# Epsilon moved into the square root's bias, and one quarter of the last token tile normalised by ScalarE and GpSimd beside VectorE

## The chip, the cores and the metric

The kernel runs on one core of one Trainium2 chip. The metric is the time of one execution in microseconds; the kernel before takes 941.61 us, the median of three runs (941.43 to 941.96).

## The reference, cut to what matters

One decoder layer: input projections, dilated window attention, a pooling mixer, gates, an output projection, and at the end a layer norm over the sum of the scaled input and the projection. The change touches only the layer norm:

```
out = jnp.einsum('bsd,de->bse', merged, w_out)
xf = DEEPNORM_ALPHA * x + out
mu = jnp.mean(xf, axis=-1, keepdims=True)
var = jnp.mean(jnp.square(xf - mu), axis=-1, keepdims=True)
y = (xf - mu) * lax.rsqrt(var + LN_EPS) * gamma + beta
```

The 256 tokens lie in two tiles of 128 partitions (t = 0 and 1); a token's row has 2048 columns, worked on as four blocks of 512 (c or b = 0 to 3).

## The kernel before, in words

Three stages stream 1 MB chunks of weights through a ring of three slots. ScalarE rounds each chunk to its high part, VectorE subtracts to get the low part, and TensorE multiplies both. Stage A makes the heads and the mixers, stage B the gates and the merged branches, stage C the output projection with its layer norm. All orders are written out by hand, one program for each engine, tied by semaphores.

In stage C, VectorE adds the scaled input to each finished block (`add_rows`), takes its statistics (`statistics`) and multiplies it by gamma at once (`times_gamma`), while TensorE works on the next block. For the last block, TensorE makes tile 0 first and then the two halves of tile 1 (`last_half`). So tile 0 is finished and stored while TensorE still computes, and what follows TensorE's last product is tile 1 alone:

- `last_half(1)`: adding the rows (L1078), statistics (L1080), `variance` with `bn_aggr` (L1089) and the addition of epsilon (L1090), and the product with gamma of the last 256 columns (L1084).
- ScalarE's square root (L808), VectorE's reciprocal (L1095) and the shift, which is minus the mean times that reciprocal (L1102).
- The shift's parts for TensorE (L1102, L1170). TensorE turns them into rows (L667), ScalarE copies these out of PSUM (L810), and TensorE multiplies them with rows of gamma and beta (L672). This gives shift times gamma plus beta of a whole block in PSUM, for blocks 1 to 3.
- VectorE makes block 0 by itself (`normalise_here`: L1110 for shift times gamma plus beta, L1112 for the result), and then blocks 1, 2 and 3 by one instruction each with the operand from PSUM (`normalise_rows`: L1119).
- SP stores each block of 256 KB as `out_ready` rises (L392), in the order of the blocks, and waits at the end until all have landed.

Ahead of the roots ScalarE loads the table for the square root by a root of a constant (L804). GpSimd has no work in this kernel.

Of the kernel before, what the change touches and what calls it, by code (L numbers as in the profile page):

```python
# [22 lines left out]
F32 = mybir.dt.float32  # L23
F32R = mybir.dt.float32r
ALU = mybir.AluOpType
ACT = mybir.ActivationFunctionType
# [14 lines left out]
LN_EPS = 1e-5  # L41
# [4 lines left out]
TT = SEQ // P  # L46
# [74 lines left out]
BLOCK = 512  # L121

ROWS = 5
BLOCKS = D_MODEL // BLOCK
BLOCK_CHUNKS = OT // BLOCKS
BLOCK_KT = KT // BLOCK_CHUNKS
# [35 lines left out]
def layer_kernel(nc, first_d, x_d, stream_d, bias_d, scale_d, gamma_d, rows_d, row_kind_d, ident_d, mask_d,  # L162
                 coef_d, inv_d, beta_d, out_d):
    with ExitStack() as ctx:
        def sem(name):
            return ctx.enter_context(nc.semaphore(name))
# [7 lines left out]
        base = nc.sbuf_base - 206 * 1024  # L174
        base = (base + 31) // 32 * 32

        def place(at, items):
            made = []
            for name, shape, dt in items:
                made.append(nc.alloc_sbuf_tensor_at(name, [P] + shape, dt, offset=at))  # L180
                at += 4 * int(np.prod(shape))
            return at, made

        at, (xt, w_raw, w_hi, w_lo, ident, coef, gate_bias, half_bias, pool_scale,
             nmax, smax, den, rden, stats, mv, rstd, shift_parts, shift,
             row_kind) = place(base, [
                 ("xt", [KT, 2, SEQ], F32R),
                 ("w_raw", [RING, CHUNK], F32), ("w_hi", [RING, CHUNK], F32R),
                 ("w_lo", [RING, CHUNK], F32R), ("ident", [P], F32),
# [2 lines left out]
                 ("nmax", [8], F32), ("smax", [8], F32), ("den", [8], F32), ("rden", [8], F32),  # L192
                 ("stats", [TT, 2 * BLOCKS, 6], F32), ("mv", [TT, 8], F32), ("rstd", [8], F32),
                 ("shift_parts", [TT, 8], F32), ("shift", [8], F32),
                 ("row_kind", [8], F32)])
        at_ya = at + (base - at) % LINE
        skew = LINE - (at_ya - at)
        at, (ya,) = place(at_ya, [("ya", [HEADS, 2, SEQ], F32R)])
# [34 lines left out]
            ("rows_hi", [D_MODEL], F32), ("rows_signed", [D_MODEL], F32)])  # L233
        _, (shift_rows, row_parts) = place(at_szp, [
            ("shift_rows", [TT, P], F32R), ("row_parts", [D_MODEL], F32R)])
        _, (last_hi, last_lo, beta, shifted) = place(base, [
            ("last_hi", [CHUNK], F32R), ("last_lo", [CHUNK], F32R), ("beta", [D_MODEL], F32),
            ("shifted", [2, BLOCK], F32)])

        _, (corr_pair, pair_f) = place(at_szp, [("corr_pair", [2, SEQ], F32), ("pair_f", [2, SEQ], F32)])  # L240
        assert max(end_a, end_b) <= nc.sbuf_usable_end, (end_a, end_b, nc.sbuf_usable_end)
# [28 lines left out]
        tail_landed = sem("tail_landed")  # L270
# [39 lines left out]
        norm_shift_ready = sem("norm_shift_ready")  # L310
        vec = sem("vec")
        var_ready = sem("var_ready")
        std_ready = sem("std_ready")
        shift_ready = sem("shift_ready")
        out_ready = sem("out_ready")
        out_landed = sem("out_landed")

        N_CONSTS = 6
        CONSTS = 16 * N_CONSTS

        block = ctx.enter_context(nc.Block())
# [41 lines left out]
        @block.sync  # L363
        def _(sp):
            def load(slot, chunk):
                sp.dma_start(w_raw[:, slot, :], stream_d[chunk, :, :]).then_inc(raw_landed[slot], 16)

            for q, (before, upto) in enumerate(PIECES):
                lies = slice(P * before * PIECE_COLS, P * upto * PIECE_COLS)
                sp.dma_start(piece_raw(q), first_d[lies].rearrange("(p c) -> p c", p=P)).then_inc(piece_landed[q], 16)  # L370
            for slot in range(RING):
                load(slot, RING + slot)
            for dst, src in ((mask[:, :, :], mask_d), (ident[:, :], ident_d), (coef[:, :], coef_d),
                             (gate_bias[:, :], bias_d), (pool_scale[:, :], scale_d), (inv[:, :, :], inv_d)):
                sp.dma_start(dst, src).then_inc(consts_landed, 16)
            whole = (CHUNKS - RING) // RING
            with sp.Fori(1, whole) as i:
                for j in range(RING):

                    sp.wait_ge(lo_split, i * (2 * RING) + 2 * (j + 1))  # L380
                    sp.dma_start(w_raw[:, j, :],
                                 stream_d[bass.ds(i * RING + (RING + j), 1), :, :]
                                 .rearrange("a p n -> (a p) n")).then_inc(raw_landed[j], 16)
            for n in range(RING * (whole + 1), CHUNKS):
                sp.wait_ge(lo_split, 2 * (n - RING + 1))
                load(n % RING, n)

            for n in range(TT * BLOCKS):

                sp.wait_ge(out_ready, n + 1)  # L390
                t, cols = n // BLOCKS, slice(n % BLOCKS * BLOCK, (n % BLOCKS + 1) * BLOCK)
                sp.dma_start(out_d[t, :, cols], res[:, t, cols]).then_inc(out_landed, 16)  # L392
            sp.wait_ge(out_landed, 16 * TT * BLOCKS)


        @block.tensor
        def _(pe):
# [268 lines left out]
            pe.wait_ge(shift_ready, 1)  # L666
            turn(value_ps[0:ROWS, 0:P], shift_parts[:, 1, 0:ROWS], ident[:, :]).then_inc(row_turned, 1)  # L667

            pe.wait_ge(rows_split, 1)
            pe.wait_ge(shift_rows_ready, 1)  # L670
            for c in range(1, BLOCKS):
                mm(norm_shift(c)[:, :], shift_rows[0:ROWS, 1, :], row_parts[0:ROWS, c * BLOCK:(c + 1) * BLOCK],  # L672
                   start=True, stop=True).then_inc(norm_shift_ready, 1)

# [2 lines left out]
        def _(act):  # L677
            activation = nc.scalar.activation
# [98 lines left out]
            with act.Fori(0, B_STEPS) as i:  # L777
                for j in range(B_CHUNKS):
                    split_hi(B_FIRST, j + AHEAD, i, B_CHUNKS)
                    correction(B_FIRST, j, i, B_CHUNKS, pair=j % 3 == 2)  # L780
                    if j % 3 < 2:
# [3 lines left out]
                                   bias=half_bias[:, bass.ds(i * 4 + ((j % 3) * OT + j // 3), 1)],  # L785
                                   scale=0.5).then_inc(tanh_done, 1)
# [13 lines left out]
            for half in range(2):  # L800
                cols = slice(half * HALF * P, (half + 1) * HALF * P)
                activation(last_hi[:, cols], w_raw[:, (CHUNKS - 1) % RING, cols], ACT.Copy).then_inc(hi_split, 1)

            activation(rstd[:, 4:5], ident[:, 0:1], ACT.Sqrt)  # L804
            for t in range(TT):

                act.wait_ge(var_ready, t + 1)
                activation(rstd[:, t:t + 1], mv[:, t, 2:3], ACT.Sqrt).then_inc(std_ready, 1)  # L808
            act.wait_ge(row_turned, 1)
            activation(shift_rows[0:ROWS, 1, :], value_ps[0:ROWS, 0:P], ACT.Copy).then_inc(shift_rows_ready, 1)  # L810


        @block.vector
        def _(dve):
            tt, ts = nc.vector.tensor_tensor, nc.vector.tensor_scalar
# [17 lines left out]
            chain = Chain()  # L833
# [233 lines left out]
                chain.add(nc.vector.bn_stats(stats[:, t, c, :], res[:, t, c * BLOCK:(c + 1) * BLOCK]))  # L1067

            def times_gamma(c, t):
                at = res[:, t, c * BLOCK:(c + 1) * BLOCK]  # L1070
                chain.add(tt(at, at, gamma[:, c * BLOCK:(c + 1) * BLOCK], ALU.mult))

# [13 lines left out]
            def variance(t):  # L1086

                chain.ready()
                chain.link(nc.vector.bn_aggr(mv[:, t, 0:2], stats[:, t, 0:BLOCKS + t, :].rearrange("p a s -> p (a s)")))  # L1089
                ts(mv[:, t, 2:3], mv[:, t, 1:2], LN_EPS, None, ALU.add).then_inc(var_ready, 1)  # L1090

            def token_rstd(t):

# [12 lines left out]
            def normalise_here(t, c):  # L1106

                cols = slice(c * BLOCK, (c + 1) * BLOCK)
                at = res[:, t, cols]
                chain.link(stt(out=shifted[:, c % 2, :], in0=gamma[:, cols], scalar=shift[:, t:t + 1],  # L1110
                               in1=beta[:, cols], op0=ALU.mult, op1=ALU.add))
                stt(out=at, in0=at, scalar=rstd[:, 2 + t:3 + t], in1=shifted[:, c % 2, :],  # L1112
                    op0=ALU.mult, op1=ALU.add).then_inc(out_ready, 1)

            def normalise_rows(t, c):

                dve.wait_ge(norm_shift_ready, c)
                at = res[:, t, c * BLOCK:(c + 1) * BLOCK]
                stt(out=at, in0=at, scalar=rstd[:, 2 + t:3 + t], in1=norm_shift(c)[:, :],  # L1119
                    op0=ALU.mult, op1=ALU.add).then_inc(out_ready, 1)  # L1120

            def split_rows():
                chain.link(copy(rows_hi[0:ROWS, :].bitcast(F32R), rows[0:ROWS, :]))
                chain.link(ts(rows_signed[0:ROWS, :], rows_hi[0:ROWS, :], row_kind[0:ROWS, 1:2], None, ALU.mult))
                stt(out=row_parts[0:ROWS, :], in0=rows[0:ROWS, :], scalar=row_kind[0:ROWS, 0:1],
                    in1=rows_signed[0:ROWS, :], op0=ALU.mult, op1=ALU.add).then_inc(rows_split, 1)

            chain.link(nc.vector.memset(shift_parts[:, :, :], 1.0))
            for e in range(OT - 1):
                if e + AHEAD < OT - 1:  # L1130
                    split_lo(C_FIRST, e + AHEAD, 0, 0)
                if e + AHEAD == OT - 1:
                    for half in range(2):
                        cols = slice(half * HALF * P, (half + 1) * HALF * P)
# [3 lines left out]
                if e % BLOCK_CHUNKS == BLOCK_CHUNKS - 1:  # L1138
                    c = e // BLOCK_CHUNKS
# [15 lines left out]
            c = BLOCKS - 1  # L1155
# [8 lines left out]
            for b in range(BLOCKS):  # L1164
# [4 lines left out]
            token_shift(1, True)  # L1169
            tt(shift_parts[:, 1, 2:3].bitcast(F32R), shift[:, 1:2], shift_parts[:, 1, 0:1],  # L1170
               ALU.subtract).then_inc(shift_ready, 1)
            normalise_here(1, 0)
            for b in range(1, BLOCKS):
                normalise_rows(1, b)


# [113 lines left out]
```

## Time and profile before

| what | value |
|---|---|
| median of the runs | 941.61 us (941.43 to 941.96) |
| span of the profiled execution, first to last instruction | 939.3 us |
| own time of the profiled execution | not recorded apart from its span |
| median of the runs less that span | 2.3 us |
| TensorE busy | 932.3 us, 99% |
| VectorE busy | 634.1 us, 68% |
| ScalarE busy | 420.2 us, 45% |
| GpSimd busy | 0.2 us, 4 instructions |
| chain that ended last | TensorE 98%, VectorE 1% |

Times in the rows count from the first instruction. A row of the timeline gives start, duration, engine, line, operation, the tile written and those read, shapes, and the number of instructions merged in it. In brackets stands the idle time before it and who ended it. Instructions on VectorE that don't wait for one another start some 0.07 us before the one in front of them ends.

### The profile page before, as it was taken

To read this page: it belongs to the slowest core of one execution; us is meant where nothing else is said; L and a number is where in the kernel's file an instruction comes from. 1 tells how busy PE (TensorE), PEld (TensorE's weight loads), DVE (VectorE), ACT (ScalarE), POOL (GpSimd) and SP (SyncE) were. 2 spreads that over 40 slices of the span, in tenths; PEclk is the share of its full clock that TensorE was granted. 3 is DMA by queue.
4 is the path that set the end of the run, shared out by engine and by line. 5 is a ranking of instruction groups with operands and counts; after the bars stand their busy time and mean duration, and the time that the engine had idled before them with its cause. 6 is when DMAs were issued, how large, how long until landed. Compare 5 with 4: busy or idle time off the path is not lost.

```text
span 939.3 us, 13719 instructions
## 1 busy us (share of the span) xinstructions
PE 932.3 (99%) x5190; PEld 812.1 (86%) x5190; DVE 634.1 (68%) x1007; ACT 420.2 (45%) x589; POOL 0.2 (0%) x4
## 2 busy tenths in 40 slices
PE   9999999999999999999999999999999999999997
PEld 7888888888888888888888889888888888888887
DVE  6767657666777567557666778666666666666866
ACT  6444444444434344444444444545445454444340
POOL 0000000000000000000000000000000000000000
PEclk9999999999999999999999999999999999999999
DMA  9745554544545545554544546655545555557432
GB/s 374 266 156 180 199 188 145 209 164 165 207 152 185 185 168 174 198 185 156 197 166 181 193 166 224 224 180 210 192 179 186 178 217 179 184 193 297 179 135 90
DMA packets 26416, 178.58 MB, mean 190 GB/s; under 512 B 3327, under 2 KB 3583, under 8 KB 5759
## 3 DMA queue, kind: packets, MB, share of 16 engines
q1 hardware_dynamic: 25920, 173.72, 51.6%
q10 hardware_dynamic: 452, 4.24, 1.2%
q8 instruction: 32, 0.52, 0.2%
q14 instruction: 12, 0.10, 0.0%
HBM read 175.85 MB, written 2.10 MB: 189 GB/s over the span
## 4 chain that ended last, share of the span: by engine, by line
PE 98%; DVE 1%; DMA 0%; ACT 0%; DVEq 0%; issue 0%
PE proj_ps L411 39%; PE proj_ps L417 20%; PE attn_ps L411 7%; PE attn_ps L403 4%; PE attn_ps L404 4%; PE attn_ps L405 4%; PE attn_ps L417 3%; PE value_ps L405 3%; PE value_ps L404 3%; PE value_ps L403 3%; PE mixed_ps L404 1%; PE mixed_ps L403 1%; PE mixed_ps L405 1%; PE mixed_ps L540 1%; PE proj_ps L454 1%; PE attn_ps L484 1%
## 5 line engine op out<-in xcount | busy, mean ns | idle before, releaser
L411 PE MATMUL proj_ps<-xt,w_hi 128*128 128x512 f32 x1600 | 557.1, 392 | 0.0
L417 PE MATMUL proj_ps<-xt,w_lo 128*128 128x256 f32 x1600 | 445.5, 280 | 0.0
L839 DVE TENSOR_TENSOR w_lo<-w_raw,w_hi 128x1024 fp32r<-128x1024 f32 x314 | 369.3, 1220 | 83.0 <-ACT w_hi L682 82.6
L411 PEld LDWEIGHTS proj_ps<-xt,w_hi 128*128 128x128 f32 x1600 | 298.3, 187 | 65.1
L682 ACT ACTIVATE w_hi<-w_raw 128x1024 fp32r<-128x1024 f32 x314 | 313.6, 1051 | 59.8 <-PE mixed_ps L405 25.1
L417 PEld LDWEIGHTS proj_ps<-xt,w_lo 128*128 128x128 f32 x1600 | 302.3, 189 | 1.4
L702 ACT ACTIVATE corr<-proj_ps 128x256 f32<-128x256 f32 x102 | 39.1, 383 | 280.8 <-PE proj_ps L417 278.2
L853 DVE TENSOR_TENSOR qk_f<-proj_ps,corr 128x256 f32<-128x256 f32 x46 | 19.5, 423 | 73.0 <-ACT corr L702 73.0
L411 PE MATMUL attn_ps<-yp,w_hi 128*128 128x512 f32 x128 | 45.1, 391 | 0.0
L411 PE MATMUL attn_ps<-ya,w_hi 128*128 128x512 f32 x128 | 45.1, 391 | 0.0
L405 PE MATMUL value_ps<-w_hi,xt 128*128 128x512 f32 x96 | 37.4, 390 | 0.0
L404 PE MATMUL attn_ps<-w_lo,xt 128*128 128x512 f32 x96 | 37.4, 390 | 0.0
L403 PE MATMUL attn_ps<-w_hi,xt 128*128 128x512 f32 x96 | 37.4, 390 | 0.0
L405 PE MATMUL attn_ps<-w_hi,xt 128*128 128x512 f32 x96 | 37.4, 390 | 0.0
L404 PE MATMUL value_ps<-w_lo,xt 128*128 128x512 f32 x96 | 37.4, 389 | 0.0
L403 PE MATMUL value_ps<-w_hi,xt 128*128 128x512 f32 x96 | 37.3, 389 | 0.0
L853 DVE TENSOR_TENSOR gate_f<-proj_ps,corr 128x256 f32<-128x256 f32 x48 | 20.3, 423 | 23.9 <-ACT corr L702 23.6
L417 PE MATMUL attn_ps<-ya,w_lo 128*128 128x256 f32 x128 | 35.8, 280 | 0.0
L417 PE MATMUL attn_ps<-yp,w_lo 128*128 128x256 f32 x128 | 35.8, 280 | 0.0
L719 ACT ACTIVATE s_sb<-s_sb,nmax 128x512 f32<-128x512 f32 x16 | 11.4, 715 | 44.7 <-DVE nmax L901 44.7
L411 PEld LDWEIGHTS attn_ps<-ya,w_hi 128*128 128x128 f32 x128 | 23.9, 187 | 5.2
L411 PEld LDWEIGHTS attn_ps<-yp,w_hi 128*128 128x128 f32 x128 | 23.9, 187 | 5.2
(178 smaller groups left out, 917.8 us busy)
## 6 DMA issues: line engine op xcount, KB each, us to landing
w_raw<-in_weights SPq DMA_DIRECT2D x158, 1024.0 KB, 4.8
first_raw<-in_first SPq DMA_DIRECT2D x8, 640.0 KB, 8.3
res<-in_x_rows ACTq DMA_DIRECT2D x1, 2048.0 KB
out_rows<-res SPq DMA_DIRECT2D x8, 256.0 KB, 2.1
gamma<-in_gamma_row ACTq DMA_DIRECT2D x1, 1024.0 KB
beta<-in_beta_row ACTq DMA_DIRECT2D x1, 1024.0 KB
mask<-in_mask SPq DMA_DIRECT2D x1, 512.0 KB, 17.7
ident<-in_identity SPq DMA_DIRECT2D x1, 64.0 KB, 17.5
```

Source lines behind the costliest of these rows:

```text
L403: mm(out, a_hi, b_hi, start=first, stop=False)
L404: mm(out, a_hi, b_lo, start=False, stop=False)
L405: return mm(out, a_lo, b_hi, start=False, stop=last)
L411: mm(bank, w_hi[:, slot, k * P:(k + 1) * P], tile.rearrange("p a s -> p (a s)"), start=first, stop=False)
L417: done = mm(bank[:, SEQ:2 * SEQ], w_lo[:, slot, k * P:(k + 1) * P], tile[:, 0, :], start=False, stop=last)
L454: mm(bank, w_hi[:, n, k * P:(k + 1) * P], xt[:, k, :, :].rearrange("p a s -> p (a s)"), start=(k == 0), stop=False)
L484: mm(out[:, :, cols], q_hi[:, g, q], keys[:, g, :, q], start=True, stop=False)
L682: activation(w_hi[:, slot, cols], w_raw[:, slot, cols], ACT.Copy).then_inc(hi_split, 1)
L702: activation(corr[:, b, :], source, ACT.Copy).then_inc(act_evac, 1)
L719: activation(s_sb[:, t, :], s_sb[:, t, :], ACT.Exp, bias=nmax[:, t:t + 1], scale=SCALE, accum_out=den[:, t:t + 1]).then_inc(exp_done, 1)
L839: tt(w_lo[:, slot, cols], w_raw[:, slot, cols], w_hi[:, slot, cols].bitcast(F32), ALU.subtract).then_inc(lo_split, 1)
L853: tt(dst, source, corr[:, bank_of(n, j), :], ALU.add).then_inc(proj_free, 1)
```

## The change

Three things are done.

- Epsilon is no longer added by VectorE (L1090 goes). A column of SBUF is set to epsilon early in stage C, and both roots take it as their bias pointer. The root now reads the variance that `bn_aggr` writes.
- Block 1 of tile 1 is not multiplied by gamma ahead (`times_gamma` leaves it out), and its rows through TensorE are left out (two products at L672 instead of three). Instead ScalarE computes block times reciprocal plus shift into a new tile, `pool_shifted`; GpSimd multiplies this by gamma and then adds beta. VectorE does blocks 0, 2 and 3.
- SP stores blocks 0, 2, 1, 3 of tile 1, in this order, and waits for GpSimd ahead of block 1.

The new column of 32 bytes moves the tiles placed behind it in SBUF by as much, but for those that are aligned anew.

```diff
@@ SP
+            def store(t, b):
+                cols = slice(b * BLOCK, (b + 1) * BLOCK)
                 sp.dma_start(out_d[t, :, cols], res[:, t, cols]).then_inc(out_landed, 16)
+            for b in range(BLOCKS):
+                sp.wait_ge(out_ready, b + 1)
+                store(0, b)
+            sp.wait_ge(out_ready, BLOCKS + 1)
+            store(1, 0)
+            sp.wait_ge(out_ready, BLOCKS + 2)
+            store(1, 2)
+            sp.wait_ge(pool_out_ready, 1)
+            store(1, POOL_BLOCK)
+            sp.wait_ge(out_ready, BLOCKS + 3)
+            store(1, 3)
@@ TensorE
-            for c in range(1, BLOCKS):
+            for c in range(POOL_BLOCK + 1, BLOCKS):
                 mm(norm_shift(c)[:, :], shift_rows[0:ROWS, 1, :], row_parts[0:ROWS, c * BLOCK:(c + 1) * BLOCK],
@@ ScalarE
-            activation(rstd[:, 4:5], ident[:, 0:1], ACT.Sqrt)
+            act.wait_ge(eps_ready, 1)
+            activation(rstd[:, 4:5], ident[:, 0:1], ACT.Sqrt, bias=eps[:, 0:1])
             for t in range(TT):
                 act.wait_ge(var_ready, t + 1)
-                activation(rstd[:, t:t + 1], mv[:, t, 2:3], ACT.Sqrt).then_inc(std_ready, 1)
+                activation(rstd[:, t:t + 1], mv[:, t, 1:2], ACT.Sqrt, bias=eps[:, 0:1]).then_inc(std_ready, 1)
+            act.wait_ge(pool_shift_ready, 1)
+            activation(pool_shifted[:, :], res[:, 1, POOL_BLOCK * BLOCK:(POOL_BLOCK + 1) * BLOCK], ACT.Identity,
+                       bias=shift[:, 1:2], scale=rstd[:, 3:4]).then_inc(centred_ready, 1)
             act.wait_ge(row_turned, 1)
             activation(shift_rows[0:ROWS, 1, :], value_ps[0:ROWS, 0:P], ACT.Copy).then_inc(shift_rows_ready, 1)
@@ GpSimd
+            pool.wait_ge(tail_landed, 16 * 5)
+            pool.wait_ge(centred_ready, 1)
+            tt(pool_shifted[:, :], pool_shifted[:, :], gamma[:, cols], ALU.mult).then_inc(pool_scaled, 1)
+            pool.wait_ge(pool_scaled, 1)
+            tt(res[:, 1, cols], pool_shifted[:, :], beta[:, cols], ALU.add).then_inc(pool_out_ready, 1)
@@ VectorE
             def times_gamma(c, t):
+                if (c, t) == (POOL_BLOCK, 1):
+                    return
@@
-                chain.link(nc.vector.bn_aggr(mv[:, t, 0:2], stats[:, t, 0:BLOCKS + t, :].rearrange("p a s -> p (a s)")))
-                ts(mv[:, t, 2:3], mv[:, t, 1:2], LN_EPS, None, ALU.add).then_inc(var_ready, 1)
+                nc.vector.bn_aggr(mv[:, t, 0:2],
+                                  stats[:, t, 0:BLOCKS + t, :].rearrange("p a s -> p (a s)")).then_inc(var_ready, 1)
@@
-                dve.wait_ge(norm_shift_ready, c)
+                dve.wait_ge(norm_shift_ready, c - POOL_BLOCK)
@@
+            nc.vector.memset(eps[:, :], LN_EPS).then_inc(eps_ready, 1)
@@
                ALU.subtract).then_inc(shift_ready, 1)
+            dve.sem_inc(pool_shift_ready, 1)
             normalise_here(1, 0)
-            for b in range(1, BLOCKS):
+            for b in range(POOL_BLOCK + 1, BLOCKS):
                 normalise_rows(1, b)
```

## Rows read from the trace of the kernel before

**Rows 1.** The page: busy time, share of the span, instructions of each engine.

```profile
PE 932.3 (99%) x5190; PEld 812.1 (86%) x5190; DVE 634.1 (68%) x1007; ACT 420.2 (45%) x589; POOL 0.2 (0%) x4
```

**Rows 2.** The chain that ended last, from 930 us: start, us, what.

```profile
930.82 0.14 PE mixed_ps L405
...
936.11 0.66 DVE res L1119
```

**Rows 3.** The timeline of VectorE from 931 us.

```profile
931.90 0.29 DVE L1089 BATCH_NORM_AGGREGATE mv<-stats 128x2 f32<-128x30 f32 x1
932.22 0.15 DVE L1090 TENSOR_SCALAR mv<-mv 128x1 f32<-128x1 f32 x1
932.29 0.41 DVE L1084 TENSOR_TENSOR res<-res,gamma 128x256 f32<-128x256 f32 x1
932.65 0.16 DVE L1095 RECIPROCAL rstd<-rstd 128x1 f32<-128x1 f32 x1
...
933.18 0.16 DVE L1170 TENSOR_TENSOR shift_parts<-shift,shift_parts 128x1 fp32r<-128x1 f32 x1
933.26 0.74 DVE L1110 SCALAR_TENSOR_TENSOR shifted<-gamma,shift,beta 128x512 f32<-128x512 f32 x1
934.04 0.75 DVE L1112 SCALAR_TENSOR_TENSOR res<-res,rstd,shifted 128x512 f32<-128x512 f32 x1
934.70 0.74 DVE L1119 SCALAR_TENSOR_TENSOR res<-res,rstd,attn_ps 128x512 f32<-128x512 f32 x1
935.36 1.40 DVE L1119 SCALAR_TENSOR_TENSOR res<-res,rstd,proj_ps 128x512 f32<-128x512 f32 x2
```

**Rows 4.** The timeline of ScalarE from 932 us.

```profile
932.41 0.20 ACT L808 ACTIVATE rstd<-mv 128x1 f32<-128x1 f32 x1 [10.81 <-DVE mv L1090]
933.71 0.27 ACT L810 ACTIVATE shift_rows<-value_ps 5x128 fp32r<-5x128 f32 x1 [1.09 <-PE value_ps L667]
```

**Rows 5.** The timeline of TensorE from 933 us.

```profile
933.40 0.28 PE L667 MATMUL value_ps<-ident,shift_parts 128*5 128x128 f32 x1 [0.16 <-DVE shift_parts L1170]
934.12 0.47 PE L672 MATMUL attn_ps<-row_parts,shift_rows 5*128 5x512 f32 x1 [0.45 <-ACT shift_rows L810]
934.43 0.62 PE L672 MATMUL proj_ps<-row_parts,shift_rows 5*128 5x512 f32 x2
```

**Rows 6.** SP's timeline, windows of the first and the last store of tile 1.

```profile
934.82 0.33 SPq L392 DMA_DIRECT2D out_rows<-res  x1
...
936.79 0.33 SPq L392 DMA_DIRECT2D out_rows<-res  x1
```

**Rows 7.** The tile res: DMAs from issue to landing.

```profile
DMA to landing us min/median/max: 2.0/2.1/2.2
```

**Rows 8.** Stretches: us, busy (x) of each engine, granted clock, DMA share, GB/s.

```profile
935.20:935.60 0.40, 0.00 (x0) 0.00 (x0) 0.40 (x2) 0.00 (x0) 0.00 (x0) 1.00 0.00 0
935.60:936.00 0.40, 0.00 (x0) 0.00 (x0) 0.40 (x1) 0.00 (x0) 0.00 (x0) 1.00 0.88 333
...
936.40:936.80 0.40, 0.00 (x0) 0.00 (x0) 0.36 (x1) 0.00 (x0) 0.00 (x0) 1.00 1.04 394
...
938.00:938.40 0.40, 0.00 (x0) 0.00 (x0) 0.00 (x0) 0.00 (x0) 0.00 (x0) 0.50 0.94 364
938.40:938.80 0.40, 0.00 (x0) 0.00 (x0) 0.00 (x0) 0.00 (x0) 0.00 (x0) 0.50 0.07 21
```

**Rows 9.** Groups by line and form: busy us, mean ns, idle before.

```profile
L784 ACT ACTIVATE th_gate<-gate_f,half_bias 128x256 f32<-128x256 f32 x32 | 16.3, 510 | 24.3 <-DVE gate_f L853 24.3
L754 ACT ACTIVATE th_gate<-gate_f 128x256 f32<-128x256 f32 x16 | 6.7, 418 | 20.6 <-DVE gate_f L853 20.6
L773 ACT ACTIVATE yp<-yp_f 128x512 fp32r<-128x512 f32 x4 | 2.5, 634 | 3.7 <-DVE yp_f L1027 3.7
L1071 DVE TENSOR_TENSOR res<-res,gamma 128x512 f32<-128x512 f32 x7 | 4.6, 687 | 0.1
L1136 DVE TENSOR_TENSOR last_lo<-w_raw,last_hi 128x1024 fp32r<-128x1024 f32 x2 | 2.4, 1218 | 0.0
L1125 DVE SCALAR_TENSOR_TENSOR row_parts<-rows,row_kind,rows_signed 5x2048 fp32r<-5x2048 f32 x1 | 2.3, 2337 | 0.0
L804 ACT ACT_TABLE_LOAD x1 | 1.3, 1283 | 0.0
```

More of the change, by code:

```diff
@@ L123 @@
 ROWS = 5
+POOL_BLOCK = 1
 BLOCKS = D_MODEL // BLOCK
@@ L185, in layer_kernel @@
              nmax, smax, den, rden, stats, mv, rstd, shift_parts, shift,
-             row_kind) = place(base, [
+             row_kind, eps) = place(base, [
                  ("xt", [KT, 2, SEQ], F32R),
@@ L194, in layer_kernel @@
                  ("shift_parts", [TT, 8], F32), ("shift", [8], F32),
-                 ("row_kind", [8], F32)])
+                 ("row_kind", [8], F32), ("eps", [8], F32)])
         at_ya = at + (base - at) % LINE
@@ L235, in layer_kernel @@
             ("shift_rows", [TT, P], F32R), ("row_parts", [D_MODEL], F32R)])
-        _, (last_hi, last_lo, beta, shifted) = place(base, [
+        _, (last_hi, last_lo, beta, shifted, pool_shifted) = place(base, [
             ("last_hi", [CHUNK], F32R), ("last_lo", [CHUNK], F32R), ("beta", [D_MODEL], F32),
-            ("shifted", [2, BLOCK], F32)])
+            ("shifted", [2, BLOCK], F32), ("pool_shifted", [BLOCK], F32)])
         _, (corr_pair, pair_f) = place(at_szp, [("corr_pair", [2, SEQ], F32), ("pair_f", [2, SEQ], F32)])
@@ L313, in layer_kernel @@
         std_ready = sem("std_ready")
+        eps_ready = sem("eps_ready")
         shift_ready = sem("shift_ready")
@@ L316, in layer_kernel @@
         out_landed = sem("out_landed")
+        pool_shift_ready = sem("pool_shift_ready")
+        pool_out_ready = sem("pool_out_ready")
+        pool_scaled = sem("pool_scaled")
+        centred_ready = sem("centred_ready")
         N_CONSTS = 6
@@ L386, in _ @@
                 load(n % RING, n)
-            for n in range(TT * BLOCKS):
-                sp.wait_ge(out_ready, n + 1)
-                t, cols = n // BLOCKS, slice(n % BLOCKS * BLOCK, (n % BLOCKS + 1) * BLOCK)
+            def store(t, b):
+                cols = slice(b * BLOCK, (b + 1) * BLOCK)
                 sp.dma_start(out_d[t, :, cols], res[:, t, cols]).then_inc(out_landed, 16)
+            for b in range(BLOCKS):
[9 more added lines that the diff above has]
+            store(1, 3)
             sp.wait_ge(out_landed, 16 * TT * BLOCKS)
@@ L802, in _ @@
                 activation(last_hi[:, cols], w_raw[:, (CHUNKS - 1) % RING, cols], ACT.Copy).then_inc(hi_split, 1)
-            activation(rstd[:, 4:5], ident[:, 0:1], ACT.Sqrt)
+            act.wait_ge(eps_ready, 1)
+            activation(rstd[:, 4:5], ident[:, 0:1], ACT.Sqrt, bias=eps[:, 0:1])
             for t in range(TT):
                 act.wait_ge(var_ready, t + 1)
-                activation(rstd[:, t:t + 1], mv[:, t, 2:3], ACT.Sqrt).then_inc(std_ready, 1)
+                activation(rstd[:, t:t + 1], mv[:, t, 1:2], ACT.Sqrt, bias=eps[:, 0:1]).then_inc(std_ready, 1)
+            act.wait_ge(pool_shift_ready, 1)
+            activation(pool_shifted[:, :], res[:, 1, POOL_BLOCK * BLOCK:(POOL_BLOCK + 1) * BLOCK], ACT.Identity,
+                       bias=shift[:, 1:2], scale=rstd[:, 3:4]).then_inc(centred_ready, 1)
             act.wait_ge(row_turned, 1)
             activation(shift_rows[0:ROWS, 1, :], value_ps[0:ROWS, 0:P], ACT.Copy).then_inc(shift_rows_ready, 1)
+        @block.gpsimd
+        def _(pool):
+            tt = nc.gpsimd.tensor_tensor
+            cols = slice(POOL_BLOCK * BLOCK, (POOL_BLOCK + 1) * BLOCK)
+            pool.wait_ge(tail_landed, 16 * 5)
[3 more added lines that the diff above has]
+            tt(res[:, 1, cols], pool_shifted[:, :], beta[:, cols], ALU.add).then_inc(pool_out_ready, 1)
         @block.vector
```

## The prediction, made before the changed kernel was run

> **What bounds the kernel now.** I read the busy shares first, then the chain of waits, then the timelines of each engine behind TensorE's last product. TensorE is busy 99% of the span [rows 1], so what VectorE and ScalarE do up to its last product is covered. The chain leaves TensorE at 930.82 + 0.14 = 930.96 us and then stays on VectorE until its last result at 936.76 or so [rows 2, 3]. Only these 8.3 us up to the span's end at 939.3 can be shortened. They are VectorE's string for tile 1, one round to ScalarE, and the last stores.
>
> The stores are the second thing to see. The first of tile 1 is issued at 934.82 and the last at 936.79 [rows 6], so the four come 0.66 us apart. One store of 256 KB at the 364 to 394 GB/s shown takes some 0.69 us, and the DMA engines are full from about 935.65 to 938.45 (share 0.88 in the first stretch, 0.94 to 1.04 behind it, 0.07 in the last) [rows 8]. VectorE's pace (0.66 us a block) and that of the stores (0.69) are the same. A faster VectorE behind the first store therefore gains next to nothing; only an earlier first store moves the end. A store lands 2.0 us or more after its issue [rows 7]; 936.79 + 2.1 = 938.89 leaves 0.38 us to the end at 939.27.
>
> **Epsilon as a bias.** L1090 goes. Before, the aggregate ended at 932.19, L1090 ran from 932.22 for 0.15, the root started at 932.41 for 0.20, and the reciprocal at 932.65 [rows 3, 4]. Each hand-over between VectorE and ScalarE is 0.04. Now the root can start at 932.23. Its bias is a pointer: a Tanh with a bias column takes 510 ns, one without 418 [rows 9], so 0.09 more, with 0 and 0.09 as the ends. Root 932.23 + 0.29 = 932.52, reciprocal at 932.56: 0.09 earlier, at the best 0.18. The gamma product (0.41) moves up with the aggregate's end and allows a start from 932.47. The early memset, and tile 0's own gain of this kind, lie under TensorE and count nothing. The same holds for the gamma product left out at block 1. The move of tiles by 32 bytes I cost at nothing: operations stay the same and most of the slack on VectorE and ScalarE is under TensorE (32% and 55% of the span idle, rows 1).
>
> So L1170 runs 933.09 to 933.25, L1110 from 933.17 to 933.91, L1112 from 933.95 to 934.70, and the first store is issued at 934.73 instead of 934.82.
>
> **What comes between on ScalarE.** The new activation is queued ahead of the copy of the rows (L810). It is released by the bare increment behind L1170, at the latest 933.29. Its price has no row: a Copy of 128x512 from SBUF is 634 ns, and two pointers at 0.09 make 0.82; the ends are 0.63 and 1.0 (two Tanh of 128x256 with a bias, rows 9). It ends at 934.11. The turned rows were ready at 933.68, the copy ran at once, and TensorE began 0.14 behind its end [rows 4, 5]. Now the copy runs 934.10 to 934.37, TensorE starts at 934.51 and gives block 2 at 934.98. VectorE would be free for it at 934.61 and waits until 935.02, 0.4 us. Block 2 ends at 935.76, block 3 at 936.42, against 936.76 for the last block before. Of the 0.66 us that one block less saves, plus 0.09, some 0.34 is left; and by the stores' pace this is worth nothing yet: 934.73 first, the second at 935.79 where 935.42 would keep the DMA engines full. The clock of TensorE is still 1.00 up to 936.80 [rows 8], so these two products are priced as before.
>
> **GpSimd.** No row shows it at work; its four instructions are 0.2 us of constants [rows 1]. The two products need a price from both sides. Below, VectorE's product of the same form: 0.69. Above, VectorE's longest instruction with two inputs here, 2.34. I take 1.22, VectorE's time for twice the columns, as if GpSimd did half of VectorE's rate [rows 9]; it is the nearest row that isn't VectorE's own price. The hand-over from ScalarE and between the two is taken as 0.04, as elsewhere.
>
> The first product could start at 934.15. Just then VectorE is in L1112, which reads two tiles of SBUF, until 934.70. Whether GpSimd runs beside such an instruction no row shows; the ends are no delay and a wait to 934.74. I take the later one, since GpSimd's own start and finish have no price at all in the sum and can only add. Then 934.74 + 1.22 + 0.04 + 1.22 = 937.22 for block 1. SP waits for it with block 3 ready behind it since 936.42. Issue at 937.26, landing 2.0 later at 939.26, block 3 behind it in the same DMA queue 0.70 later at 939.96, and 0.38 to the end: 940.34. That is 1.07 us more than 939.27. The profiled span lies 2.3 us under the median, and its own time is not known; I take the same 2.3 around it after: 941.61 + 1.07 = 942.7 us.
>
> The Trainium skill speaks to both choices (SBUF — State Buffer, Who interferes with whom): a VectorE instruction with two SBUF inputs and a GpSimd instruction that reads SBUF exclude each other, and the later one is blocked for the whole instruction. The sum by it is the one above, 942.7; without it it would be 942.1. No row here shows it. The skill's GpSimd page (GPSIMD Engine Reference, Elementwise — side-by-side cycle accounting) gives 4497 ns for 2048 columns of a two-input sum on GpSimd; an estimate from it is about 1.12 us for 512 columns, and the sum would be 942.5.
>
> **The rivals.**
> Side by side: GpSimd isn't held back. It ends at 934.15 + 2.48 = 936.63, is issued at 936.67, and the end is 936.67 + 2.0 + 0.70 + 0.38 = 939.75: 942.1 us. For it: nothing in the trace shows an engine slowed by another. Against it: nothing shows GpSimd at all.
>
> GpSimd at VectorE's own rate, 0.69 each, unhindered: block 1 is ready at 935.57, before block 2. Then the stores set the end: first landing 936.73, block 2 at 937.79, then 938.49 and 939.19, end 939.57. If ScalarE's activation is also at its lower end and the wait for the rows is short, the four land 0.70 apart from 936.73, and the end is 939.2. 941.5 to 941.9 us. This is the most that the change can gain, about 0.1 us, because the first store moves by only 0.09 to 0.18.
>
> Slower: GpSimd becomes the bound by more than the measurement's error. It is one mechanism: block 3's store is queued behind the wait for block 1, so each microsecond that the pair ends behind some 936.2 comes out as one microsecond. At 2.34 each the pair ends at 939.46, and the time is 944.9. It counts as slower (over 943.5) once the pair ends behind 938.03, at 1.62 us a product. A first instruction on GpSimd that has to be fetched or started up would act the same way. For it: an engine idle for 939 us and no price. Against it: its four constants took their 0.1 us each without any sign of that.
>
> ScalarE loads another table for the activation: 1.28 us [rows 9] ahead of it, and it carries the copy of the rows with it. GpSimd then starts at 935.43, past L1112, and ends at 937.91; 943.4 us. Against it: the Copy at L810 ran behind the root without a load.
>
> **How the numbers follow.** The forecast gets 0.38, side by side 0.25, GpSimd near VectorE's rate 0.14, GpSimd as the bound far out 0.16, the table 0.04, and 0.03 for a gain by something not seen here. The predicted time is 942.7. The range from 941.3 to 944.2 takes in the lower rivals and half of the slow one. A measurement of this kernel can tell about 0.2% from no change, 1.9 us: faster means under 939.7, slower over 943.5. Nothing that the change touches can give 1.9 us; faster 0.03. Slower 0.16 and a little of the forecast's and the table's upper tails: 0.20. The rest, 0.77, is the same.
>
> **What would show it.** The reciprocal of tile 1 should start some 0.09 us earlier behind TensorE's last product, and the first of the last stores as well. The new activation should last about 0.8 us with the copy at L810 directly behind it, and VectorE should idle some 0.4 us ahead of block 2. GpSimd's two rows give their own price, and the start of the first against the end of L1112 shows which of the first two cases it is. SP should wait for GpSimd, and the last two issues should be 0.33 apart. The prediction is wrong if the pair ends ahead of VectorE's block 3, if TensorE's last product moves by more than 0.3 us, or if the last store isn't issued behind GpSimd's.

## The result: 952.0 us, slower by 10.4 us

The changed kernel takes 952.0 us, the median of six runs (951.91 to 952.14). The ratio to the kernel before is 1.009 (95% interval 1.0066 to 1.0114). The forecast was 942.7 with a range up to 944.2, and the time lies far outside.

The executions of the kernel before fall into two groups, here and below, most near 941.3 us and some near 946.3, and what makes them comes out below. Its median was 941.61 us over the first three runs and 941.79 over all six (two of them in the upper group); the 10.4 us are counted from the first.

From the page of the changed kernel, its span and part 1:

```profile
span 950.4 us, 13721 instructions
PE 941.9 (99%) x5189; PEld 813.0 (86%) x5189; DVE 632.9 (67%) x1004; ACT 421.0 (44%) x590; POOL 3.2 (0%) x6
```

The span is 11.1 us longer, and TensorE is busy 9.6 us longer with one product less [rows 1]. So the loss lies mostly where the change did nothing. The tail is what follows TensorE's last product of the projection. By engine (the timelines of VectorE, ScalarE, TensorE, GpSimd and SP; columns as in [rows 3]):

```profile
940.99 0.42 DVE L1115 SCALAR_TENSOR_TENSOR res<-res,mixed_ps 128x256 f32<-128x256 f32 x1 [1.82 <-PE mixed_ps L424]
...
941.91 0.29 DVE L1126 BATCH_NORM_AGGREGATE mv<-stats 128x2 f32<-128x30 f32 x1
942.12 0.36 DVE L1121 TENSOR_TENSOR res<-res,gamma 128x256 f32<-128x256 f32 x1
942.57 0.16 DVE L1132 RECIPROCAL rstd<-rstd 128x1 f32<-128x1 f32 x1
...
943.10 0.16 DVE L1208 TENSOR_TENSOR shift_parts<-shift,shift_parts 128x1 fp32r<-128x1 f32 x1
943.23 0.75 DVE L1147 SCALAR_TENSOR_TENSOR shifted<-gamma,shift,beta 128x512 f32<-128x512 f32 x1
944.01 0.75 DVE L1149 SCALAR_TENSOR_TENSOR res<-res,rstd,shifted 128x512 f32<-128x512 f32 x1
944.78 1.41 DVE L1156 SCALAR_TENSOR_TENSOR res<-res,rstd,proj_ps 128x512 f32<-128x512 f32 x2
...
942.24 0.29 ACT L828 ACTIVATE rstd<-mv,eps 128x1 f32<-128x1 f32 x1 [10.71 <-DVE mv L1126]
943.17 0.81 ACT L830 ACTIVATE pool_shifted<-res,shift,rstd 128x512 f32<-128x512 f32 x1 [0.63 <-DVEq L1210]
943.89 0.25 ACT L833 ACTIVATE shift_rows<-value_ps 5x128 fp32r<-5x128 f32 x1
...
944.28 0.70 PE L691 MATMUL proj_ps<-row_parts,shift_rows 5*128 5x512 f32 x2 [0.70 <-ACT shift_rows L833]
...
944.13 1.76 POOL L843 TENSOR_TENSOR pool_shifted<-pool_shifted,gamma 128x512 f32<-128x512 f32 x1 [943.68 <-ACT pool_shifted L830]
945.97 1.26 POOL L845 TENSOR_TENSOR res<-pool_shifted,beta 128x512 f32<-128x512 f32 x1
...
944.79 0.33 SPq L396 DMA_DIRECT2D out_rows<-res  x1
...
947.26 0.81 SPq L396 DMA_DIRECT2D out_rows<-res  x2
```

TensorE's last product ends at 940.98 (the chain has it at 940.84 for 0.14), against 930.96 before: 10.0 us later. From there to the span's end it is 9.4 us, against 8.3 before [rows 2]. The tail went as the sum had it; 10 us came from ahead of it.

Where they come in, three landmarks show that are the same instructions in both kernels. They are ScalarE's Tanh in stage A, its Tanh in stage B, and the ten products by which TensorE is kept busy behind its last one. Each row gives the shortest, median and longest duration, and the first and last start; first the kernel before, then the changed one:

```profile
L754 ACT ACTIVATE th_gate<-gate_f x16: 416/418/419, 70.6 to 571.8; 128x256 f32<-128x256 f32 x16
L784 ACT ACTIVATE th_gate<-gate_f,half_bias x32: 509/509/511, 587.4 to 838.7; 128x256 f32<-128x256 f32 x32
...
L665 PE MATMUL value_ps<-last_hi,merged x10: 388/389/397, 930.8 to 932.8; 128*128 128x512 f32 x10
```

```profile
L773 ACT ACTIVATE th_gate<-gate_f x16: 417/418/419, 70.8 to 576.8; 128x256 f32<-128x256 f32 x16
L803 ACT ACTIVATE th_gate<-gate_f,half_bias x32: 508/510/512, 592.3 to 848.6; 128x256 f32<-128x256 f32 x32
...
L684 PE MATMUL value_ps<-last_hi,merged x10: 388/389/398, 940.8 to 942.9; 128*128 128x512 f32 x10
```

Stage A takes 506.0 us between its first and last Tanh instead of 501.2, and stage B 256.3 instead of 251.3. From B's last Tanh to the start of the last of the ten products it is 94.3 us instead of 94.1. So 4.8 us are lost in A and 5.0 in B, and next to nothing in C. TensorE's groups in stage B (window 600 to 840 us; mean duration in ns behind the busy time), before and then changed:

```profile
L411 PE MATMUL proj_ps<-xt,w_hi 128*128 128x512 f32 x462 | 160.8, 391 | 0.0
L417 PE MATMUL proj_ps<-xt,w_lo 128*128 128x256 f32 x462 | 129.4, 280 | 0.0
```

```profile
L430 PE MATMUL proj_ps<-xt,w_hi 128*128 128x512 f32 x456 | 161.7, 399 | 0.0
L436 PE MATMUL proj_ps<-xt,w_lo 128*128 128x256 f32 x456 | 128.0, 281 | 0.0
```

In stages A and B most of the work is done by pairs of products, one pair for each 128 rows of a chunk of weights: 512 columns with the high weights, 256 with the low ones. TensorE doesn't wait between them, the clock is the same (0.999 over the span in both), and yet a pair takes longer: the 48 chunks of stage B are 768 pairs, and 5.0 us over 768 is 6.5 ns each. From start to start a pair takes 346.7 ns before and 353.3 after. I call these the fast and the slow pace. The timelines show the difference in shape (starts in us), before and then changed:

```profile
699.89 0.39 PE L411 MATMUL proj_ps<-xt,w_hi 128*128 128x512 f32 x1
700.12 0.28 PE L417 MATMUL proj_ps<-xt,w_lo 128*128 128x256 f32 x1
700.24 0.39 PE L411 MATMUL proj_ps<-xt,w_hi 128*128 128x512 f32 x1
700.47 0.28 PE L417 MATMUL proj_ps<-xt,w_lo 128*128 128x256 f32 x1
700.59 0.39 PE L411 MATMUL proj_ps<-xt,w_hi 128*128 128x512 f32 x1
```

```profile
700.11 0.40 PE L430 MATMUL attn_ps<-yp,w_hi 128*128 128x512 f32 x1
700.35 0.28 PE L436 MATMUL attn_ps<-yp,w_lo 128*128 128x256 f32 x1
700.47 0.40 PE L430 MATMUL proj_ps<-xt,w_hi 128*128 128x512 f32 x1
700.71 0.28 PE L436 MATMUL proj_ps<-xt,w_lo 128*128 128x256 f32 x1
700.82 0.40 PE L430 MATMUL proj_ps<-xt,w_hi 128*128 128x512 f32 x1
```

Before, each short product starts 0.23 us behind its long one. Changed, that distance runs through 0.24, 0.24 and 0.23 and then again: three pairs in 1.06 us instead of 1.04.

### The profile page after: what moved, and what is told of

It is laid out like the page before. It is cut to its first block, busy times and chain, and to the rows that moved or that the text cites. A ratio compares the mean times of both kernels' runs of the same rounds, so it can differ in the third digit from the quotient of the medians.

```text
span 950.4 us, 13721 instructions
## 1 busy us (share of the span) xinstructions
PE 941.9 (99%) x5189; PEld 813.0 (86%) x5189; DVE 632.9 (67%) x1004; ACT 421.0 (44%) x590; POOL 3.2 (0%) x6
## 4 chain that ended last, share of the span: by engine, by line
PE 98%; DMA 0%; ACT 0%; POOL 0%; DVE 0%; POOLq 0%; issue 0%
PE proj_ps L430 39%; PE proj_ps L436 20%; PE attn_ps L430 7%; PE attn_ps L422 4%; PE attn_ps L423 4%; PE attn_ps L424 4%; PE attn_ps L436 3%; PE value_ps L422 3%; PE value_ps L424 3%; PE value_ps L423 3%; PE mixed_ps L424 1%; PE mixed_ps L422 1%; PE mixed_ps L423 1%; PE mixed_ps L559 1%; PE proj_ps L473 1%; PE attn_ps L503 1%
## 5 line engine op out<-in xcount | busy, mean ns | idle before, releaser
L430 PE MATMUL proj_ps<-xt,w_hi 128*128 128x512 f32 x1600 | 565.2, 398 | 0.0
```

The costliest lines, as they stand in the source:

```text
L430: mm(bank, w_hi[:, slot, k * P:(k + 1) * P], tile.rearrange("p a s -> p (a s)"), start=first, stop=False)
```

## The experiments

Ratios are to the kernel before on the same chip, with 95% intervals.

**Which part costs the 10 us.** Four kernels.

`e1_eps_only` has the epsilon part alone: the column `("eps", [8], F32)` behind `row_kind`, both roots with `bias=eps[:, 0:1]`, L1090 gone.

> The kernel before with only the epsilon part: the column of 32 bytes, both roots with a bias pointer, L1090 gone. In the changed kernel TensorE's last product ended 10.0 us later than before, and the pairs of products in stages A and B came every 353.3 ns instead of 346.7. Theory 'placement' (the 32 bytes that move the tiles behind them set TensorE's pace): the pairs at 353 ns and about 951.5 us. Theory 'GpSimd' (a GpSimd that is configured or waits through the run sets it): 347 ns and 941.5 us. Theory 'any edit' (the pace falls out anew with each program): either, and not the same in the four kernels sent together.

`e2_quarter_only` is the changed kernel without that part.

> The changed kernel without its epsilon part: no column of 32 bytes, L1090 stays, block 1 of tile 1 by ScalarE and GpSimd. Theory 'GpSimd': TensorE's pairs every 353 ns, last product near 941, about 952.1 us. Theory 'placement': 347 ns, and only the tail's loss of 1.1 us less the 0.09 of the epsilon part, so 942.9 us.

`e3_tile_only`:

```diff
-                 ("row_kind", [8], F32)])
+                 ("row_kind", [8], F32), ("eps", [8], F32)])
```

> The kernel before with the unused column of 32 bytes and nothing else, so that only places in SBUF differ. Theory 'placement': pairs at 353 ns, 951.6 us. Theory 'GpSimd': 347 ns, 941.6 us.

`e4_pool_waits`:

```diff
+        @block.gpsimd
+        def _(pool):
+            pool.wait_ge(tail_landed, 16 * 5)
```

> The kernel before with a GpSimd program that only waits for the loads of stage C (its one wait lasts some 870 us) and computes nothing. Theory 'GpSimd' in the form that its waiting costs TensorE: pairs at 353 ns, 951.6 us. In the form that the configuration for its arithmetic costs: 941.6 us. Theory 'placement': 941.6 us.

Measured: 951.0 (1.0102, 1.0082 to 1.0122), 942.2 (1.0012, 1.0002 to 1.0021), 951.2 (1.0107, 1.009 to 1.0124) and 941.6 us (1.0008, 0.999 to 1.0025), where the kernel before had 941.1. In e1 one of four runs took 1323.59 us at a mean granted clock of 0.655, where the others have 0.999 and more; no trace of it is kept, and why the clock fell is not known. It is left aside, and the other three lie within 0.3 us. The unused column alone costs 10.1 us. A GpSimd that waits costs nothing, and the quarter costs the 1.1 us of the tail. 'Placement' holds, and the parts add up: 10.1 and 1.1, less some 0.2 for epsilon (e1 against e3, whose own runs differ by 0.8), make 11.0; seen are 10.4 us between the medians and 11.1 between the spans.

**Which tiles.**

> The epsilon part alone, as in e1, but the column lies in a gap ahead of ya, so that no other tile moves. The unused column alone had cost 10 us. Theory 'placement': pairs at 347 ns again, TensorE's last product near 931, and 0.1 to 0.2 us less than before from the earlier root, 941.0 us. A rival, that the bias pointer or the read of a new tile costs something in itself: 951 us as e1.

> The kernel before with the tiles of stage A alone (queries, keys, values, scores, probabilities, pool inputs) 32 bytes further on, the gates' tiles unmoved. TensorE reads these in its short products between the chunks of pairs. Theory 'entry' (the pairs' pace is chosen by how the last short products ended, so by tiles that TensorE itself reads): slow pairs as with the column, 951 us. Theory 'evacuation' (the pace hangs on ScalarE's and VectorE's tiles corr and gate, which run beside the pairs): unmoved, 941.5 us.

> The other half: only the tiles from szp to sum_f lie 32 bytes off (back instead of on, the same place in a line of 64 bytes), stage A's tiles unmoved. Theory 'entry': 941.5 us. Theory 'evacuation': 951 us, pairs at 353 ns.

> The unused column made 64 bytes. If what counts is a tile's place within 64 bytes, the moved tiles lie as before: pairs at 347 ns and 941.5 us. If any other place than the old one does it: 951 us or another time between the two.

The edits:

```diff
f1  +        _, (eps,) = place(at, [("eps", [8], F32)])      # ahead of ya, nothing else moves
f2  -        at_phase = at
    +        at_phase = at + 32
f3  -        at_szp = at + skew
    +        at_szp = at + skew - 32
    (and at_phase = at + 32, which is its old place)
f4  +        ("eps", [16], F32)                              # in place of [8], unused
```

Measured: f1 941.3 us (1.0002, 0.9986 to 1.0018), f2 950.9 (1.0097, 1.0065 to 1.0129), f3 941.5 (0.9999, 0.9978 to 1.0019), f4 950.9 (1.0097, 1.0065 to 1.0129). Stage A's tiles do it. 64 bytes do it as well as 32, so a tile's place within 64 bytes isn't what decides. The expected 0.1 to 0.2 us for epsilon in f1 can't be told from nothing.

The profiled executions of f1 and f3 fell in the second group (946.32 and 946.59 us). Stage A is there as in the kernel before, but in stage B the group in f1 reads

```profile
L414 PE MATMUL proj_ps<-xt,w_hi 128*128 128x512 f32 x457 | 162.1, 399 | 0.0
```

with the 399 ns of the slow pace, where the kernel before has 391. So the two groups are one program whose stage B runs at the fast or the slow pace as a whole; 768 pairs by 6.6 ns are the 5.0 us between them. (Of the kernel before itself only an execution of the lower group has a trace; in f1 nothing is moved, and eight of its ten executions are in the lower group.)

The traces show where the two groups part: ahead of stage B, at the last short products of stage A (the pool map), whose program begins with waits. Before and then f1:

```profile
569.15 0.28 PE L417 MATMUL proj_ps<-xt,w_lo 128*128 128x256 f32 x1
569.37 0.36 PE L403 MATMUL attn_ps<-p_hi,w_hi 128*128 128x256 f32 x1
```

```profile
569.41 0.28 PE L420 MATMUL proj_ps<-xt,w_lo 128*128 128x256 f32 x1
569.62 0.36 PE L406 MATMUL attn_ps<-p_hi,w_hi 128*128 128x256 f32 x1
```

From start to start it is 217 ns before and 206 in f1, and from here on the distances differ. In the nine traces of kernels with all tiles that TensorE reads in their old place and no needless product, it is 217 to 232 ns in the five with a fast stage B (before, e2, e4, h1, m4) and 205 to 213 in the four with a slow one (f1, f3, g1, m3). So some ns at this one wait go with the pace of the 768 pairs behind it. That they cause it no run shows, and what varies them isn't known.

**Is the place itself slow, or is a pace entered and kept?** In both kernels the pace changes only where TensorE does something else than pairs. The kernel before has slow stretches too: single chunks of 16 pairs, at 64, 140, 216, 423 and 499 us, and seven chunks from 288 to 351 us. In a part of the last the changed kernel is at the fast pace (window 296 to 318 us, before and then changed):

```profile
L411 PE MATMUL proj_ps<-xt,w_hi 128*128 128x512 f32 x64 | 22.7, 399 | 0.0
```

```profile
L430 PE MATMUL proj_ps<-xt,w_hi 128*128 128x512 f32 x65 | 22.6, 391 | 0.0
```

The pairs read the weights and xt, in every third chunk of stage B ya and yp instead, and no edit has moved these: ya and yp are aligned anew behind the column. This spoke for a pace that is entered and then kept, 'entry' for short.

> The kernel with the unused 32-byte column (951 us, slow pairs through stage B) with one needless product of 128x512 into an idle bank, between the last mix and stage B. It costs some 0.2 us itself. Theory 'entry' (the pace at which the pairs lock is taken from what TensorE did just before and is then kept): stage B can lock at 347 ns, which is 764 pairs by 6.6 ns = 5.0 us less, 946.2 us. If the place of tiles acts on the pairs themselves: 951.4 us with stage B at 353 ns. An entry that still locks slow would also give 951.4 and would leave it open.

> The kernel before with 32 bytes ahead of mixed_corr: of stage A's tiles only those that TensorE never reads move (mixed_corr, silu_za, qk_f, u_pad, pool_a, pool_b, inv). Theory 'entry by TensorE's own reads': 941.5 us. Theory 'ScalarE's and VectorE's timing': 951 us or some part of the 10 us.

> 32 bytes ahead of s_sb: the scores s_sb and the probabilities pt move with the tiles of h1, queries, keys and values stay. If the mix's reads of pt (or the turns' of s_sb) choose the pace: 951 us. If the queries, keys or values do: 941.5 us.

> The whole change, but with epsilon's column in the gap ahead of ya, so that nothing moves. If placement was all of the 10 us, what is left is the tail: GpSimd's products took 1.76 and 1.26 us and end 1.1 us later than the old last store allowed, so 942.2 to 942.5 us with pairs at 347 ns. If the placement and the GpSimd work act together in some way: over 945 us.

The edits:

```diff
k1  +            mm(value_ps[:, :], xt[:, 0, 0, 0:P], xt[:, 0, :, :]..., start=True, stop=True)   # ahead of stage B
h1  +                    ("pad", [8], F32), ("mixed_corr", [SEQ], F32)
h2  +                    ("pad", [8], F32), ("s_sb", [TT, KEYS], F32)
```

k1 has the unused column and the needless product: 951.5 us (1.0086, 1.0053 to 1.0119), stage B still slow, which by itself left it open. h1: a median of 946.1, but its ten runs are four near 941.2 and six near 946.3, the two groups of the kernel before, and its profiled one (941.04 us) has the kernel before's pace in every stretch; the ratio is 1.0017 (0.9991 to 1.0043). h2: 951.1 us (1.0088, 1.0058 to 1.0118). So the tiles of stage A that TensorE never reads don't matter, and a move of s_sb and pt is enough. g1: 942.1 to 942.95 in five runs and 947.1 to 948.2 in five, the two groups again, with the tail's 1.1 us on each.

> The kernel with the unused column (stage B at 353 ns a pair) with a needless product ahead of each chunk of stage B but the first, of 32, 64, 96, 128, 160, 192, 256, 320, 384, 448 and 512 columns in this order, in each of the four turns of the loop. Theory 'entry' (a pace once taken is kept until another kind of work comes between): after some of the lengths the next chunks run at 347 ns, after others at 353, changing only at chunk borders and alike in the four turns. If the place of tiles acts on the pairs directly: 353 ns throughout. The added products cost up to 6 us, so the total says little; the pace in each chunk is what counts.

```diff
+                    if j:
+                        cols = (0, 32, 64, 96, 128, 160, 192, 256, 320, 384, 448, 512)[j]
+                        mm(value_ps[:, 0:cols], xt[:, 0, 0, 0:P], xt[:, 0, :, :]...[:, 0:cols], start=True, stop=True)
```

The kernel takes 954.4 us (one run), the needless products in it. The pace of each chunk, from the starts of its products, in ns a pair:

```
columns ahead   none   32   64   96  128  160  192  256  320  384  448  512
turn 1          353   353  347  347  353  353  353  353  347  347  347  347
turns 2 to 4    347   347  347  353  353  353  353  353  347  347  347  347
```

Two neighbouring chunks of the first turn, behind 96 and behind 128 columns (windows 599.4 to 604 and 605 to 609.7 us):

```profile
L411 PE MATMUL proj_ps<-xt,w_hi 128*128 128x512 f32 x14 | 4.9, 394 | 0.0
...
L411 PE MATMUL proj_ps<-xt,w_hi 128*128 128x512 f32 x14 | 5.0, 399 | 0.0
```

(394 and 391 ns both go with 346.7 ns from start to start, 399 with 353.3.) In one loop, with no tile moved between its turns, the pace changes at a chunk's border behind one odd product (64, 96, 128 and 320 columns did it), and is kept when nothing comes between (512 columns in one turn to none in the next). That is shown. Which way a given product throws it hangs on more than its length and the pace before it: behind a fast chunk, 96 columns kept the fast pace in turn 1 and ended it in turns 2 to 4.

> 32 bytes ahead of pt: of the tiles that TensorE reads only the probabilities pt move, s_sb stays. If the mix's reads of pt choose the pace: 951 us, as with both moved. If the turns' reads of s_sb do: 941 or 946 us, as before.

The edit is the pad of h2 ahead of pt instead of s_sb. 951.4 us (1.0091, 1.006 to 1.0122), with stage B at the slow pace (window 600 to 840 us):

```profile
L411 PE MATMUL proj_ps<-xt,w_hi 128*128 128x512 f32 x457 | 162.0, 399 | 0.0
```

Moving pt and what lies behind it is enough, and h1 has cleared what lies behind. It is the place of the probabilities, which TensorE reads in the mix, the short products just ahead of a run of pairs. The first mix shows it at work. In the kernel before and in m2 the chunk ahead of it runs at the same distances, to the ns, up to the mix's first product; within the mix the two part. The mix's next to last product, before and then m2:

```profile
70.65 0.46 PE L540 MATMUL mixed_ps<-pt,v_hi 128*128 128x512 f32 x1
```

```profile
70.65 0.44 PE L540 MATMUL mixed_ps<-pt,v_hi 128*128 128x512 f32 x1
```

From the start of each product to the next start, in ns:

```
         ahead of the mix   the mix's twelve products                          the pairs behind it
before   120 236 123        229 117 118 60 170 59 168 58 170 59 293 118        233 124 229 117 230
m2       120 236 123        232 116 118 62 174 57 173 60 167 60 282 118        229 117 231 118 240
```

Behind it the pairs are fast before and slow in m2. (ScalarE and VectorE write pt, so that their writes have a part in it isn't excluded.) And pt isn't the only tile whose place counts: in e3, where queries, keys and values lie further on too, the distance just ahead of the first mix is already another, 113 ns and not 123, and the fast stretches of stage A lie elsewhere (284 to 324 us, in m2 274 to 288). The time is nearly the same.

> The version that the runs point to: the epsilon part alone with its column in the gap (nothing moved, no GpSimd), and one needless product of 320 columns ahead of stage B, 0.15 us. In the survey a product of 320 columns always left the pairs at 347 ns. The kernel before enters stage B at 347 or at 353 ns, by execution (941.3 or 946.3 us). Theory 'entry': all executions near 941.3 us. If the entry hangs on more than the product just ahead: still two groups.

> The kernel with the unused 32-byte column (951.2 us, pairs at 353 ns in most stretches) and a needless product of 320 columns behind each of the seven mixes of stage A and ahead of stage B, 1.2 us in all. Theory 'entry': the stretches behind them run at 347 ns although the tiles lie where they cost 10 us; were all of them cured, 951.2 - 10.0 + 1.2 = 942.4 us; stage B alone, 947.4. If the place acts itself: 952.4 us.

The edits: 320 columns of the survey's product, in n1 ahead of stage B, in n2 there and behind each mix of stage A. n1: 946.3 us (1.0054, 1.004 to 1.0068), all five runs in the upper group, where the kernel before had one of eleven beside it. My expectation that 320 columns always lead to the fast pace fell: the product led to the slow one. In the trace the last mix ahead of it still runs as in the kernel before, to 1 ns, which without the product goes over into a fast stage B. n2: 944.6 us (1.0036, 1.0023 to 1.005), 6.6 us less than e3 although eight products were added. Behind the same product that n1 has there, stage B is fast here; it takes 251.5 us between its Tanh, as before the change:

```profile
L789 ACT ACTIVATE th_gate<-gate_f,half_bias x32: 509/510/513, 590.8 to 842.3; 128x256 f32<-128x256 f32 x32
```

The tiles lie where they cost 10 us, and 6.6 us of it are gone by entries alone. Stage A ran as in the kernel before up to 286 us, and from 354 to 566 us it was slow again but for two chunks (window 360 to 392 us):

```profile
L411 PE MATMUL proj_ps<-xt,w_hi 128*128 128x512 f32 x92 | 32.5, 399 | 0.0
```

No version here beats the kernel before: f1 equals it.

**GpSimd's first product.**

> The whole change with nothing moved, and GpSimd's first product held until VectorE has finished block 0, so that VectorE runs only instructions with one operand in SBUF beside it. Theory 'shared reads' (the 1.77 us of the first product against 1.26 of the second is waiting for VectorE's two-operand instructions): 1.26 us for both. Theory 'first call' (the first of its kind on GpSimd is slow) or 'the product is dearer than the sum': still 1.77. The end: start at 934.9 and 2.6 or 3.1 us, so 942.3 or 942.8 us where stage B is fast.

> The whole change with nothing moved, and one needless product on GpSimd early in stage C, some 60 us ahead of the two that count. Theory 'first call': the early one takes 1.8 us or more and the one that counts 1.26 us, 0.5 us gained. Theory 'shared reads': the one that counts still 1.77, for VectorE's two-operand instructions run beside it as before; the early one 1.26 if VectorE is idle beside it.

```diff
m3  +            pool.wait_ge(out_ready, BLOCKS + 1)         # behind centred_ready
m4  +            tt(pool_shifted[:, :], gamma[:, cols], gamma[:, cols], ALU.mult).then_inc(pool_warm, 1)
```

GpSimd's timeline, m3 and then m4:

```profile
940.02 1.27 POOL L846 TENSOR_TENSOR pool_shifted<-pool_shifted,gamma 128x512 f32<-128x512 f32 x1 [939.58 <-DVE res L1152]
941.37 1.26 POOL L848 TENSOR_TENSOR res<-pool_shifted,beta 128x512 f32<-128x512 f32 x1
```

```profile
854.26 1.04 POOL L846 TENSOR_TENSOR pool_shifted<-gamma 128x512 f32<-128x512 f32 x1 [853.81 <-DMA row_kind<-in_row_kind]
934.60 1.71 POOL L849 TENSOR_TENSOR pool_shifted<-pool_shifted,gamma 128x512 f32<-128x512 f32 x1 [79.30 <-ACT pool_shifted L834]
936.39 1.26 POOL L851 TENSOR_TENSOR res<-pool_shifted,beta 128x512 f32<-128x512 f32 x1
```

Held until VectorE is past its instruction with two operands in SBUF, the first product takes 1.27 us; warmed up 80 us earlier it still takes 1.71. 'Shared reads' holds, 'first call' falls. VectorE's own instruction kept its 0.75. The Trainium skill (SBUF — State Buffer, Who interferes with whom) says that a VectorE instruction with two inputs in SBUF contends with a GpSimd instruction that reads SBUF, and that the one that comes later is blocked until the other ends. The trace agrees nearly: in the changed kernel VectorE's L1149 runs 0.63 us into the product, which takes 0.49 us longer than the held one of m3 (1.76 against 1.27). Holding it back gains nothing: m3 has 942.4 to 943.3 us in its lower group, g1 942.1 to 942.95.

## Why the prediction was wrong

The step that failed is one sentence of it: "The move of tiles by 32 bytes I cost at nothing: operations stay the same and most of the slack on VectorE and ScalarE is under TensorE". The slack of those two engines was the wrong cover to name. The move touches TensorE's own operands, TensorE had hardly any slack (99% busy, [rows 1]), and its pairs fell into the slow pace in most stretches of A and in all of B: the unused column alone measured 10.1 us. No rival held it. One sign of being wrong was named and came: a last product of TensorE that moves by more than 0.3 us; it moved by 10.0 us. The trace of the kernel before could have warned: it shows both paces, 391 and 399 ns for the same group, and that would have priced the whole risk: some 1,600 pairs at the fast pace in A and B, by 6.6 ns, are 10.6 us.

The rest of the sum held: the handing over of the quarter was forecast to cost 1.07 us with epsilon's 0.09 gained, and costs 1.1 where nothing is moved (g1; e2 has 1.1 without epsilon). Point by point, counted from TensorE's last product:

- Epsilon. The reciprocal followed the aggregate's start by 0.66 us instead of 0.75 [rows 3]: 0.09, as forecast, with the root at 0.29. The first store is issued 3.81 us behind the last product instead of 3.86 [rows 6]. The bare increment on VectorE takes back some 0.05, which I had not counted.
- ScalarE's activation: 0.81 us, forecast 0.82. It began 0.07 us behind the start of L1208, not 0.20, and the copy of the rows began 0.09 us ahead of its end, so VectorE's expected 0.4 us of idling ahead of block 2 shrank to some 0.1: L1156 starts 0.77 us behind L1149, where 0.66 lay between such instructions before. The last block ends at 946.19, 5.21 behind the last product, forecast 5.46, before 5.80.
- GpSimd: the end of its pair was forecast 6.26 us behind the last product and is 6.25 (947.23). That is luck in part, for two errors cancel: the start was 3.15 and not 3.78 behind, and the products took 1.76 and 1.26 instead of 1.22 twice. That the wait for VectorE is real is shown; that it lies inside the instruction's row I had not expected.
- The stores: the last two are issued 0.48 apart (0.81 less 0.33), behind GpSimd, and the end is 9.4 us behind the last product, forecast 9.38. What VectorE gained, 0.59 us, is lost behind GpSimd: the wait of the stores for GpSimd was forecast rightly.

What stays open is the mechanism inside TensorE: why the place of pt or an odd product chooses between two steady paces of the same pairs, and whether the some 10 ns at the pool map's wait are the cause of the two groups or go with it. A rule from which a fast entry could be built was not found.

## What to carry to other kernels

On a kernel that TensorE bounds, compare the time of TensorE's repeated groups before and after a change to anything, and first test a new tile alone, unused: it takes one line, and here it was the whole result. Put small new tiles into gaps, so that nothing else moves. A quarter of VectorE's last work handed to GpSimd costs 2.5 us where VectorE takes 0.74, and 3.0 if VectorE reads two tiles beside it, and with the DMA engines already full behind the first store [rows 8] there was next to nothing to win by it.

## What the hardware showed that I had not expected

- Alternating products of 512 and 256 columns have two steady paces on TensorE at full granted clock, 346.7 and 353.3 ns a pair (1.9%), kept over the 768 pairs and some 270 us of stage B, and in no trace here left but where other products come between.
- A move of tiles that the pairs don't read can change the pace: pt by 32 bytes (9.9 us), the tiles of stage A and the gates by 32 or 64 (10.1 and 9.7). So can one product ahead of them (of 64, 96, 128 and 320 columns in the survey).
- GpSimd's two-input product of 128x512 takes 1.26 to 1.27 us beside VectorE instructions with one SBUF operand, 1.04 with one tile as both inputs, and 0.15 us pass between the end of ScalarE's activation and the start of the first product (943.98 to 944.13).
